# Down-projection weights loaded as one 8 KB run per partition, with matching strided transposes

## What is computed

```python
for e in range(N_EXPERTS):                       # 32
    a = clamped_swiglu(t @ w_gate_up[e] + b_gate_up[e])   # 1024 -> 2048 -> 1024
    out = out + combine[:, e:e + 1] * (a @ w_down[e] + b_down[e])   # 1024 -> 1024
```

## Time and profile before

| | |
|---|---|
| median of three runs | 1402.73 us |
| lowest, highest | 1400.97, 1403.94 us |
| span of the profiled execution | 1398.9 us |
| TensorE busy | 1269.9 us (91%) |
| VectorE busy | 435.9 us (31%) |
| ScalarE busy | 324.2 us (23%) |
| GpSimd busy | 116.0 us (8%) |
| moved by DMA | 453.46 MB, mean 324 GB/s |

### The profile page before, as it was taken

How to read it: one execution, slowest core, us unless ns; L and a number is a source line. 1 busy time by engine, 2 the same in 40 slices (tenths; PEclk the granted TensorE clock), 3 DMA queues, 4 the chain that set the end, 5 groups by cost and what they waited for, 6 DMA issues and landing times.

```text
span 1398.9 us, 18538 instructions
## 1 busy us (share of the span) xinstructions
PE 1269.9 (91%) x7222; PEld 675.9 (48%) x7222; DVE 435.9 (31%) x917; ACT 324.2 (23%) x554; POOL 116.0 (8%) x81
## 2 busy tenths in 40 slices
PE   6999996888979999999999899999989999989996
PEld 5999985777973323333333333333333333323332
DVE  4966446463631212212121221212122121222213
ACT  4673444543421101011011101101110110111111
POOL 1301444452000000000000000000000000000000
PEclk9999998899979999999999999999999999999999
DMA  6647432122878799999999999999999999999991
GB/s 205 200 122 239 122 121 91 61 91 89 314 275 340 283 416 405 419 408 417 408 411 420 418 418 416 414 406 408 420 409 418 417 417 417 402 420 413 417 410 69
DMA packets 122709, 453.46 MB, mean 324 GB/s; under 512 B 12112, under 2 KB 55248, under 8 KB 89872
## 3 DMA queue, kind: packets, MB, share of 16 engines
q1 hardware_dynamic: 120992, 451.31, 81.7%
q10 hardware_dynamic: 1680, 1.64, 0.4%
HBM read 451.87 MB, written 1.05 MB: 324 GB/s over the span
## 4 chain that ended last, share of the span: by engine, by line
PE 82%; DVE 7%; ACT 7%; issue 2%; DMA 1%; SPq 1%; POOL 0%; DVEq 0%; ACTq 0%
PE psum L973 32%; PE psum L995 18%; PE psum L697 8%; PE psum L694 8%; PE psum L941 4%; PE psum L965 4%; PE psum L648 4%; DVE ZS L1709 2%; DVE HT L1712 2%; ACT L1242 1%; ACT ZS L1242 1%; ACT HT L1244 1%; DMA ring<-in_w_in_dram 1%; DVE AMX L1567 1%; PE psum L858 1%
## 5 line engine op out<-in xcount | busy, mean ns | idle before, releaser
L1704 DVE TENSOR_SCALAR ZS<-psum 128x512 f32<-128x512 f32 x32 | 22.1, 691 | 744.0 <-PE psum L973 744.0
L995 PE MATMUL psum<-ring,HT 128*64 128x512 f32 x896 | 219.0, 644 | 22.0 <-ACT HT L1244 22.0
L973 PE MATMUL psum<-ring,ZS 128*64 128x512 f32 x1024 | 225.2, 592 | 0.0
L973 PE MATMUL psum<-slot,ZS 128*64 128x512 f32 x768 | 170.2, 592 | 0.0
L973 PEld LDWEIGHTS psum<-ring,ZS 128*64 128x64 f32 x1024 | 73.5, 137 | 146.2 <-issue 146.2
L995 PEld LDWEIGHTS psum<-ring,HT 128*64 128x64 f32 x896 | 66.1, 147 | 154.4 <-issue 124.8
L1240 ACT ACTIVATE QT<-psum 128x256 f32<-128x256 f32 x32 | 12.3, 384 | 488.6 <-PE psum L648 488.6
L973 PEld LDWEIGHTS psum<-slot,ZS 128*64 128x64 f32 x768 | 55.1, 137 | 109.7 <-issue 109.7
L1287 DVE TENSOR_TENSOR WL<-ring,WH 128x2048 fp32r<-128x2048 f32 (+1 forms) x30 | 68.0, 2267 | 52.1 <-ACT WH L1030 52.1
L1030 ACT ACTIVATE WH<-ring 128x2048 fp32r<-128x2048 f32 (+1 forms) x42 | 78.7, 1873 | 19.9 <-DMA ring<-in_w_in_dram 15.2
L1246 ACT ACTIVATE HT<-psum 128x512 f32<-128x512 f32 x32 | 19.1, 597 | 249.7 <-PE psum L995 249.7
(11 more groups left out here) (302 smaller groups left out, 1360.8 us busy)
## 6 DMA issues: line engine op xcount, KB each, us to landing
ring<-in_w_gate_up_dram SPq DMA_DIRECT2D x128, 1024.0 KB, 10.6
ring<-in_w_down_dram SPq DMA_DIRECT2D x112, 1024.0 KB, 16.7
slot<-in_w_gate_up_dram SPq DMA_DIRECT2D x96, 1024.0 KB, 7.9
XDT<-in_w_gate_up_dram SPq DMA_DIRECT2D x32, 1024.0 KB, 6.0
ring<-in_w_in_dram SPq DMA_DIRECT2D x30, 1024.0 KB, 5.4
XC<-in_w_down_dram SPq DMA_DIRECT2D x16, 1024.0 KB, 20.3
ring<-in_w_branch_ssm_dram SPq DMA_DIRECT2D x4, 1024.0 KB, 4.9
ring<-in_w_branch_nsa_dram SPq DMA_DIRECT2D x4, 1024.0 KB, 4.9
```

Of the source, the lines that this page charges most:

```text
L973: ins = mm(psum[64 * (c % 2):64 * (c % 2) + 64, c // 2, :], XTS[:, k, s], w[:, 512 * c:512 * c + 512], start=False, stop=(k == KT - 1))
L995: ins = mm(psum[64 * h:64 * h + 64, 2, :], lhs, w[:, 1024 * (k % 2) + 512 * h:1024 * (k % 2) + 512 * h + 512], start=(k == 0), stop=(k == ...
```

## The change

The DRAM side of a down unit's load is read in another order: partition p gets rows 2p and 2p+1 of the unit's 256, which are neighbours in memory, in place of rows p and 128+p. Its two halves of the slot therefore hold the even rows and the odd rows. To match, the transposes take every second column of `ABU`: transpose `jb` starts at column 256 * (jb // 2) + jb % 2 and steps by 2, in place of 128 neighbouring columns. The products at L995 are not edited.

```diff
                 else:
-                    src = w_down[0, e, 256 * (j - 8):256 * (j - 8) + 256, :].rearrange("(k p) n -> p k n", p=P)
+                    src = w_down[0, e, 256 * (j - 8):256 * (j - 8) + 256, :].rearrange("(p k) n -> p k n", k=2)
                     dst = dst.rearrange("p (k n) -> p k n", k=2)
                 sp.dma_start(dst, src).then_inc(slot_full[slot_of(s, j)], 16)
...
                     for jb in range(4):
-                        ins = tr(bank(7, 4, P)[:, jb], ABU[:, P * jb:P * jb + P])
+                        first = 256 * (jb // 2) + jb % 2
+                        ins = tr(bank(7, 4, P)[:, jb], ABU[:, first:first + 255:2])
                     ins.then_inc(at_full, 1)
```

## The result

The changed kernel took 1407.36 us in the median of 7 runs (1406.39 to 1411.24), the kernel before 1402.26 (1400.21 to 1405.91, also 7 runs). The ratio is 1.0045, with a 95% interval of 1.003 to 1.0059. So it is 5.1 us slower, clear of no change and inside the stated range of 1400.5 to 1412, but not what the forecast held likeliest. The span grew from 1398.9 to 1404.7.

What follows compares the result with a forecast made beforehand. The prediction took TensorE's own program, products plus the wait for the activation, as the bound, not transfers. Terms 0 + 0 + 0 on a 1398.9 us span plus 3.8 gave 1402.7, stated as 1403; range 1400.5 to 1412.

Steps and rivals of the forecast that it cites:

- Parts 1 and 2: Down loads with 16,384 fewer packets, and their issue on SyncE: both hidden by early landing and queue waiting, each 0.
- rival B: Expert loads: transfers do limit somewhere and fewer packets free them; 16 us faster, 1387; chance 0.03.
- Part 3: Transposes of ABU on the path: weight loads reading every second float taken as 0, upper bound 19.7 us.
- rival A: Four transposes between L1712 and L1244: each strided weight load costs 73 ns more, 9.3 us in all, 1412; chance 0.26.
- rival A': Same transposes: only the first strided load is exposed, the others hide under products; 2.3 us, 1405; chance 0.09.
- Part 4: TensorE's clock falling to 1.2 GHz at L995: pattern should stay; one or two events either way, 1.5 to 3 us.
- the sum: Whole kernel: three terms of 0 on a span of 1398.9, plus 3.8 us, gives 1402.7, stated as 1403.
- Rival C: Clock at L995: two to three fewer low-clock events, 3 to 4.5 us faster, 1399; chance 0.07.
- Rival D: Down loads: rows still go as separate 4 KB packets, count stays 122,709; time 1403 or rival A's; chance within the forecast's 0.54.

Runs made afterwards that it cites:

- dma_only: Kernel before with only the load changed (8 KB runs), transposes still reading neighbouring columns; 1402.01 us, ratio 1.0.
- the fill pair: Kernel before, and perm2, each with two unneeded products ahead of TensorE's activation wait in each pair's first expert; 1383.44 and 1384.69 us.
- the tab pair: Kernel before, and perm2, each with a one-column sigmoid behind the token copies, moving ScalarE's table load; 1377.2 and 1369.24 us.
- perm2: Changed kernel, but transposes read neighbouring columns; VectorE's clamps reorder while reading PSUM at step 4 and write in sequence; 1403.24 us, ratio 1.0003.
- step8: Kernel before with transposes reading every eighth column, running on into the tile behind the activation; 1405.53 us, ratio 1.0028.
- stride_only: Kernel before with only the transposes changed to every second column, loads still two 4 KB runs; 1409.56 us, ratio 1.0051.
- step4: Kernel before with transposes reading every fourth column; 1409.32 us, ratio 1.0054.
- fifth: Kernel before with the fourth transpose done twice in every expert, no strided read; 1410.35 us, ratio 1.0055.
- perm: Changed kernel, but transposes read neighbouring columns; VectorE's clamps reorder by writing in turn to places 128 floats apart; 1414.09 us, ratio 1.0081.
- fill_before: Kernel before with two unneeded products ahead of TensorE's activation wait in each pair's first expert; 1383.44 us, ratio 0.9856.
- tab_perm2: perm2 with a one-column sigmoid behind the token copies, moving ScalarE's table load to idle time; 1369.24 us, ratio 0.976.

## Why the prediction was right and where it was wrong

Parts 1 and 2, the loads and their issue at 0: right, shown by dma_only. That busy transfers were no limit was read from the waits and from the slack, and the loads were indeed covered. The prediction had the rate too, 29.96 us an expert at 420 GB/s against 30.46 taken, but used it only to price rival B, and not to say how near the limit was: 30.46 us an expert is 413 GB/s, and the loads brought 418 where they did limit. A pair of 59.45 us (the fill pair) still ran on the units loaded ahead; at 58.12 us (the tab pair) the loads became the bound, and the part priced at 0 was worth 8 us.

Part 3 is the step that failed. It took 0 for the strided weight loads because "Step 2 is nearer to step 1 than to step 8" and because VectorE's L1704 "pays nothing". The bounds were right, the choice was not: steps 2, 4 and 8 cost 69, 72 and 52 ns a load, so nearness to step 1 did not count, and the read of another engine from another memory said nothing about this one. The rows held the hint, and rival A names it: a transpose's load does 128 columns in 140 ns, about what L799 needs for 64, so it had something to lose (an ordinary load of 128 takes 192). What came is near rival A', 73 x 32 = 2.3 us, with 2.8 measured; each load grew by 69 ns, four by 276, and the group of four by 88, so a third of the growth shows.

A weight of 0.09 on A' was too little, and A, at four times 73 ns, too much: loads that overlap were added up.

The rule that the prediction took from the Trainium skill ("SBUF — State Buffer", section "Specifications (TRN2)") does not fit these loads in either half. Step 2 has the two hits in a line of 16 bytes that full bandwidth is said to want, and pays 69 ns. Step 8 crosses to a new line with every column, twice as often as step 2, and pays less, 52 ns.

Part 4, the clock: the mechanism was right, its size was left open. It was put at "one or two events either way" around 0 and as an addition to A. (The two windows of the earlier trace rows do not begin at the same point of the expert, so they do not hold quite the same work; 7.09 against 8.56 us for the same 32 products bears the reading out.) It turned out the larger half of the loss, 3.3 us against 2.8. In these runs it has one sign, too: dma_only and perm2, with the stretch as before, have 219.2 us of L995 and again 12 events, and each kernel with a longer stretch has more: 220.9 in step8, 222.3 in the changed kernel, stride_only and step4, 224.0 in fifth, 226.1 in perm. The events follow a rhythm: in the kernel before the first, sixth, eleventh and sixteenth pair stay without one, and a pair with one takes up to 61.15 us; in the changed kernel only the first and the twelfth do, and it takes up to 61.33 us. What sets the rhythm was not tested, so that longer means more is what these lengths show and no rule. Rival C, fewer events by chance, finds no support: kernels whose loops have the same lengths have the same events, in three traces (12; the loop 938.8 to 939.1 us) and in three more (14; 945.0 to 945.1).

One more reading of part 4 was wrong. It took the spread of the runs for one or two such events. The loops of the kernel before, dma_only and perm2 take 938.8, 939.1 and 939.1 us, while they begin at 440.0, 444.4 and 441.8: the spread of these executions lies ahead of the loop. And the 3.8 us that the sum adds to the span are not all time around it. In each timed run the device time is 1.7 us above that run's span; the other 2.1 say that the profiled execution was a fast one.

The chances gave "slower" 0.31 and "same" 0.59; the range of 1400.5 to 1412 held the time, because part of the way to the upper bound of part 3 had been kept in it. That the number fell inside does not bear the forecast out: its own range, 1400.5 to 1405, missed, and what came is A' with two events more, which the prediction had named and held unlikely. Rival D did not happen.

## What to carry to other kernels

An access pattern that makes a transfer tidier is paid for where the data is read; take the reorder to an instruction that does it for nothing (perm2), and try its inner run both ways round. On a path that repeats, price a stretch by what it does to the clock as well: 88 ns an expert cost as much again in half-clock products. And before calling transfers hidden, put the loop's demand beside the rate that they reach when they limit: with 413 of 418 GB/s in use, the loop could gain some 20 us elsewhere (fill_before), and with the next gain the transfers became the bound.

## What the runs showed of the hardware that was not expected

- A transposed weight load of 128 neighbouring float columns takes 140 ns, an ordinary one 192. Read with a step of 2, 4 or 8 columns, it takes 209, 212 and 192.
- TensorE's granted clock fell to 1.2 GHz at L995 behind waits of only 2.04 and 0.69 us with 0.66 us of transposes between them, in 12 of 16 pairs, for 19.7 us in all. 1.93 us of filling work, or a first wait of 0.71 us, removed every event.
- ScalarE loads a table twice in each iteration of the loop, 1.28 us each time: ahead of the token copies (L1221), where it has nothing else to do, and ahead of the first sigmoid (L1242), where TensorE waits. A one-column sigmoid right behind the token copies moves the second load off the path; both loads remain.
- VectorE takes 1056 ns in place of 691 when it writes in turn to two places 128 floats apart; reading PSUM with a step of 4 floats in runs of 128 costs it nothing.
- Expert loads held 418 GB/s with the down weights in 4 KB packets and 422 with all in 8 KB, in the fill and the tab pair alike.
- The best version found, tab_perm2, is 2.4% faster than the kernel before (ratio 0.976, 0.9742 to 0.9778).
